# Which column pairs use the seven-product scheme, which PSUM banks they and their neighbours take, and where the input forms are built: one transformer kernel on one core

## The chip, the core and the metric

The kernel runs on one NeuronCore of a Trainium2 chip. Five engines work side by side: TensorE (PE, with its weight loads shown apart as PEld), VectorE (DVE), ScalarE (ACT), GpSimd (POOL) and SyncE (SP, here the queue that issues the weight transfers). Each runs its own instruction list in order and waits on semaphores for the others. PSUM has eight banks of 128 x 512 float32 words; a matmul writes into a bank, ACT and DVE read it out. The metric is the device time of one execution in microseconds (us), the median of several runs.

## The reference, cut to what matters

Two transformer blocks are computed on 512 tokens of width 1024, in float32. The change touches three of the SwiGLU feed-forward layers of the second block:

```python
def _swiglu(x, w_in, w_out):
    a, b = jnp.split(x @ w_in, 2, axis=-1)      # w_in: 1024 x 5632, a = gate, b = val
    return (jax.nn.silu(a) * b) @ w_out          # w_out: 2816 x 1024
# per layer l:
n = _modulate(_rmsnorm_2(h, norm_g[l, 0]), mod[:, 0, 0], mod[:, 0, 1])
h = h + 0.5 * mod[:, 0, 2] * _swiglu(n, ffn_w_in[l, 0], ffn_w_out[l, 0])
# ... the mixer ...
n = _modulate(_rmsnorm_2(h, norm_g[l, 2]), mod[:, 2, 0], mod[:, 2, 1])
h = h + 0.5 * mod[:, 2, 2] * _swiglu(n, ffn_w_in[l, 1], ffn_w_out[l, 1])
```

There are four such layers. The three that the change touches are called s01 (layer 0, second), s10 and s11 (layer 1, first and second).

## The kernel before, in words

**Number format.** Every float32 operand of a matmul is split into a high part and a rest (`HH`/`HL` for the layer's input, `AH`/`AL` for the activations, `wh`/`wl` for weights), and a product takes three matmuls: high x high, high x rest, rest x high. The weights come as slabs of 128 x 1024 (eight blocks of 128 x 128). SP loads slab n into one of five buffers `st`; `Act.split` copies it to `wh` (one of three), and `Dve.split` subtracts to get `wl`. Both are called by `spend`, two slabs ahead of TensorE, and `wh` of slab n waits until TensorE has used slab n-3.

**The up projection.** The 2816 columns of gate and val are taken in 22 groups g of 128, in 11 pairs p = 0 to 10 (g = 2p and 2p+1). In a plain pair, `linear` computes gate g, val g, gate g+1, val g+1, each one slab, 24 matmuls over all 512 tokens, into a bank of its own. ACT then takes the SiLU of gate (which frees gate's bank), DVE multiplies by val (which frees val's bank), ACT writes the high half to `AH`, DVE the rest to `AL`. Pair 0 is special: `three_linear` computes gate 0, val 0 and gate 1 together in two token halves, since the norm is still being finished, and then comes val 1.

**The fast pairs.** The pairs of `FAST` are computed by `fast_pair` with a Strassen-like scheme: columns g and g+1, and the even and odd 128-row blocks of the input, form a 2 x 2 block product in seven steps in place of eight, each step 24 matmuls over 256 words. The order is `FORMS`: 11, 12, s2, s1, s3, s4, 22. Its four weight slabs are combined by DVE sums (`Z`, and three sums in place in `st`) inside `Dve.split`. Four of the steps (s2, s1, s3, 22) need sums of the input, the input forms: `Dve.input_forms` builds `TF` 0 to 3 from the normalised input and then their rests `TL`, `Act.input_forms` the high parts `TH`. The results of gate and val gather in three banks each, by role: A (four steps), B (one), E (two). ACT copies partial results out (`kept`), DVE adds. The last output of a pair, from bank A, is finished by a closure `tail`, called by `finish_pair`, which frees the two A banks: gate's by a SiLU on ACT, val's by a product on DVE (line 2233).

**Halves.** `PARTS` = ((0, 12), (12, 10)): pairs 0 to 5, then a down projection over 12 groups, then pairs 6 to 10 and a down projection over 10 groups. Both down projections are eight plain linears over `AH`/`AL`.

**Banks.** `Pe.bank(key, ring)` takes the next bank of a ring, with one counter for each ring, which is never reset; `Pe.claim` makes TensorE wait until the bank's last holder is freed. Before, plain linears, the three of pair 0 and the down projection all use the ring (0, 1, 2, 3, 4), and fast pairs take six banks in turn from the ring 0 to 7. TensorE works in order, so a bank that is not free stops everything behind it.

**Order on DVE and ACT.** For each plain g, `fast_swiglu` does: `spend(8)` (not for g = 1), `finish_pair`, the forms where they are due, `spend(8)`, the SiLU or product, high half and rest. In g = 0 all four forms and their four rests stand around the second `spend`.

Of the kernel before, what the change touches and what calls it, by code (L numbers as in the profile page):

```python
# [19 lines left out]
DFF = 2816  # L20
# [2 lines left out]
NWS = 3  # L23
HID = 11
PARTS = ((0, 12), (12, 10))
FAST = (1, 3, 5, 7, 9)
FORMS = ("11", "12", "s2", "s1", "s3", "s4", "22")
NC = 8
RESET = 256
# [4 lines left out]
def c128(start):  # L34
    return np.arange(start, start + 128)
# [139 lines left out]
def finish(steps):  # L175
    for _ in steps:
        pass
# [277 lines left out]
class Pe:  # L455
# [590 lines left out]
    def fast_pair(self, key, p, up):  # L1046


        m, w = self.m, self.w
        g, n0, r0 = 2 * p, self.cur.at // 8, len(self.specs) // 8  # L1050
        for row, k in ((0, 0), (0, 1), (1, 0), (1, 1)):
            self.specs += [(*up, c128((2 * i + k) * 128), c128(at + (g + row) * 128)) for at in (0, DFF) for i in range(4)]
        self.plan += [(kind, r0) for kind in FORMS]
        self.freed += [("sum", n0 + 5), ("lo", n0 + 5), ("lo", n0 + 4), ("lo", n0 + 6)]
        self.cur.at += 56
        ring = tuple(range(8))

        def plain_form(k, h):
            return [[t[2 * i + k][:, part(h)] for i in range(4)] for t in (m.HH, m.HL)]

        def turned_form(t):
            w.wait_ge("form lo", key, t)
            return [[a[t][:, 256 * i:256 * i + 256] for i in range(4)] for a in (m.TH, m.TL)]

        for step, kind in enumerate(FORMS):
            n = n0 + step
            w.wait_ge("lo", n)
            s = n % NWS
            hi, lo = plain_form(*{"11": (0, 0), "12": (1, 0), "s4": (1, 1)}[kind]) if kind in ("11", "12", "s4") else turned_form(("s1", "s2", "s3", "22").index(kind))
            for x, name in enumerate(("gate", "val")):  # L1070
                bank = ("A", "B", "A", "E", "A", "E", "A")[step]
                out = (key, name, bank, g)
                if step in (0, 1, 3):
                    b = self.bank(out, ring)
                else:
                    b = m.ps[self.banks[out]]
                    w.wait_ge("kept", key, g, x, (None, None, 0, None, 1, 2, 3)[step])
                for i in range(4):
                    cols = slice(512 * x + 128 * i, 512 * x + 128 * i + 128)
                    wh, wl = m.wh[s][:, cols], m.wl[s][:, cols]  # L1080
                    self.mm(b[:, 0:256], wh, hi[i], i == 0 and step in (0, 1, 3), False)
                    self.mm(b[:, 0:256], wh, lo[i], False, False)
                    self.mm(b[:, 0:256], wl, hi[i], False, i == 3, *([("q", key, g, x, step)] if i == 3 else []), *([("used", n)] if x and i == 3 else []))

    def fast_ffn(self, key, after, up, down):
        m = self.m
        dense = (0, 1, 2, 3, 4)

        def one(name, g):
            finish(self.linear((key, name, g), fe(c128((0 if name == "gate" else DFF) + g * 128), *up, 8), m.HH, m.HL, None, dense))  # L1090

        for half, (first, count) in enumerate(PARTS):
            self.w.stamp("pe ffn", key, half)
            for p in range(first // 2, (first + count) // 2):
                if p == 0:
                    self.three_linear([(key, "gate", 0), (key, "val", 0), (key, "gate", 1)], [fe(c128(at), *up, 8) for at in (0, DFF, 128)], m.HH, m.HL, key, dense)
                    one("val", 1)
                elif p in FAST:
                    self.fast_pair(key, p, up)
                else:  # L1100
                    for g in (2 * p, 2 * p + 1):
                        one("gate", g)
                        one("val", g)
            if half:
                self.w.stamp("inputs free", after)
            for i in range(8):
                specs = [(down[0], down[1], c128((first + j) * 128), c128(i * 128)) for j in range(count)]
                ready = [("lo", key, "f", first + j) for j in range(count)]
                if half and i == 7:
                    self.last_linear((key, "down", half, i), specs, m.AH, m.AL, ready, dense, after)  # L1110
                else:
                    finish(self.linear((key, "down", half, i), specs, m.AH, m.AL, ready, dense))
            self.pad()

    def mixer(self, l):
# [229 lines left out]
class Act:  # L1345
# [590 lines left out]
    def fast_pair(self, key, p, j):  # L1936
        m, w, g = self.m, self.w, 2 * p

        def keep(step, k, bank):
            for x, name in enumerate(("gate", "val")):  # L1940
                w.wait_ge("q", key, g, x, step)
                self.act(m.kept[x][k], self.ps(key, name, bank, g)[:, 0:256], ACT.Copy, ("kept", key, g, x, k))

        for step in range(7):
            finish(self.spend(8))
            if step == 0:
                self.finish_pair()
            if step in (0, 2, 3, 4):
                keep(step, {0: 0, 2: 1, 3: 2, 4: 3}[step], "E" if step == 3 else "A")
        w.wait_ge("c1", key, g, 0)  # L1950
        self.act(m.c1[0], m.c1[0], ACT.Silu, (key, "silu", g))
        w.wait_ge(key, "f", g)
        self.half((key, "f", g), m.c1[0], m.AH[j])

        def tail():
            if g >= 2:
                w.wait_ge("lo", key, "f", g - 1)
            w.wait_ge("q", key, g, 0, 6)
            self.act(m.y2[:, part(0)], self.ps(key, "gate", "A", g)[:, 0:256], ACT.Silu, ("free", (key, "gate", "A", g)), scale=-1.0)
            w.wait_ge("c22", key, g, 0)  # L1960
            self.act(m.y2[:, part(1)], m.c22[0], ACT.Silu, (key, "silu", g + 1), scale=-1.0)
            w.wait_ge(key, "f", g + 1)
            self.half((key, "f", g + 1), m.y2, m.AH[j + 1])

        self.tail = tail

    def fast_swiglu(self, key, after, l, sub):
        m, w = self.m, self.w
        self.high_halves(key, self.shift(l, sub))
        forms = self.input_forms(key)  # L1970
        for half, (first, count) in enumerate(PARTS):
            for p in range(first // 2, (first + count) // 2):
                if half:
                    w.wait_ge("pe ffn", key, half)
                if p in FAST:
                    self.fast_pair(key, p, 2 * p - first)
                    continue
                for g in (2 * p, 2 * p + 1):
                    if g != 1:
                        finish(self.spend(8))  # L1980
                    self.finish_pair()
                    if g == 0:
                        next(forms)
                        next(forms)
                    finish(self.spend(8))
                    if g == 0:
                        finish(forms)
                    y = m.f[0 if g % 2 else 2]
                    w.wait_ge(key, "gate", g)
                    if g >= 2:  # L1990
                        w.wait_ge("lo", key, "f", g - 2)
                    self.act(y, self.ps(key, "gate", g), ACT.Silu, ("free", (key, "gate", g)), (key, "silu", g))
                    w.wait_ge(key, "f", g)
                    w.wait_ge("pe ffn", key, half)
                    self.half((key, "f", g), y, m.AH[g - first])
            self.finish_pair()
            self.down(after, half, count)
# [215 lines left out]
class Dve:  # L2213
# [714 lines left out]
            self.tail()  # L2928
            self.tail = None

    def fast_pair(self, key, p, j):
        m, w, g = self.m, self.w, 2 * p

        def summed(out, kept, x, name, bank, step, *points):
# [3 lines left out]

        for step in range(7):
            finish(self.spend(8))  # L2940
            if step == 0:
                self.finish_pair()
            for x, name in enumerate(("gate", "val")):
                if step == 1:
                    summed(m.c1[x][:, part(0)], 0, x, name, "B", 1)
# [20 lines left out]
    def fast_swiglu(self, key, after, l, sub):  # L2966
        m, w = self.m, self.w
        self.adanorm(key, l, sub)
        forms = self.input_forms(key, l, sub)
        for half, (first, count) in enumerate(PARTS):  # L2970
            for p in range(first // 2, (first + count) // 2):
                if p in FAST:
                    self.fast_pair(key, p, 2 * p - first)
                    continue
                for g in (2 * p, 2 * p + 1):
                    if g != 1:
                        finish(self.spend(8))
                    self.finish_pair()
                    if g == 0:
                        next(forms)  # L2980
                        next(forms)
                    finish(self.spend(8))
                    if g == 0:
                        finish(forms)
                    y = m.f[0 if g % 2 else 2]
                    w.wait_ge(key, "silu", g)
                    w.wait_ge(key, "val", g)
# [482 lines left out]
```

## Time and profile before

| | before |
|---|---|
| runs | 3354.31, 3357.98, 3357.48 us |
| median | 3357.48 us |
| profiled execution | 3356.16 us, span 3354.4 us |
| granted TensorE clock, mean | 0.992 |
| busy: PE / PEld / DVE / ACT / POOL | 98% / 81% / 60% / 41% / 4% of the span |

The span is the time from the first to the last instruction of the profiled execution. "Busy" is the union of an engine's instructions. A row of the wait or timeline views ends with the idle time before the instruction and, after an arrow, what ended it. PEclk, or granted clock, is the share of TensorE's full clock (2.4 GHz) that was granted; half of it is 1.2 GHz.

### The profile page before, as it was taken

What the parts mean: (1) busy time and instruction counts of PE and PEld (TensorE: products, weight loads), DVE (VectorE), ACT (ScalarE), POOL (GpSimd) and SP (SyncE); (2) the same over time, 40 slices, a digit from 0 to 9 for tenths busy, and PEclk for the clock granted to TensorE, in tenths of its full rate; (3) what the DMA queues carried; (4) which work ended last, traced back from release to release, by engine and by line L of the source; (5) the groups of instructions that cost most, each with busy time, mean ns of one, the idle gap of its engine ahead of it and who ended that gap; (6) DMA issues with size and microseconds to landing.
All of it is one profiled execution on the core that took longest, in us unless ns stands there. A gap on an engine that the chain in (4) does not pass through costs nothing.

```text
span 3354.4 us, 49836 instructions
## 1 busy us (share of the span) xinstructions
PE 3277.8 (98%) x21186; PEld 2730.3 (81%) x21186; DVE 2008.2 (60%) x3327; ACT 1391.4 (41%) x2352; POOL 118.7 (4%) x211
## 2 busy tenths in 40 slices
PE   8999999999999999999999899999999999999998
PEld 6878768888888888887778788889898877888897
DVE  6575764678576756566645654566364566475454
ACT  5234566345244422235543442344243455343242
POOL 1000000101000011100000000000000000000000
PEclk9999999999999999999999899999999999999999
DMA  4010103655543466632112132323333321222332
GB/s 153 25 58 30 39 32 122 217 175 202 181 139 132 151 217 212 224 131 94 45 64 94 63 109 93 101 65 106 113 101 121 100 68 45 84 80 76 113 101 69
DMA packets 101742, 364.28 MB, mean 109 GB/s; under 512 B 11776, under 2 KB 13888, under 8 KB 100880
## 3 DMA queue, kind: packets, MB, share of 16 engines
q1 hardware_dynamic: 77040, 272.14, 24.4%
q0 software_dynamic: 24480, 88.95, 7.8%
q8 instruction: 167, 2.74, 0.3%
q14 instruction: 55, 0.45, 0.0%
HBM read 358.94 MB, written 2.10 MB: 108 GB/s over the span
## 4 chain that ended last, share of the span: by engine, by line
PE 90%; DVE 6%; ACT 3%; issue 1%; DMA 0%; POOL 0%; DVEq 0%; ACTq 0%; POOLq 0%
PE ps_run L478 89%; PE ps_run L870 1%; DVE wl L2226 1%; ACT wh L1358 1%; ACT nrm L1358 1%; DVE TF L2233 0%; DVE TL L2226 0%; DVE nrm L2233 0%; PE ps_run L1208 0%; DVE HL L2233 0%; DVE msk L2230 0%; ACT bias L1358 0%; DVE nrm L2226 0%; DVE X L2233 0%; ACT HH L1358 0%
## 5 line engine op out<-in xcount | busy, mean ns | idle before, releaser
L2226 DVE TENSOR_TENSOR wl<-st,wh 128x1024 fp32r<-128x1024 f32 x541 | 658.8, 1218 | 654.3 <-ACT wh L1358 654.2
L478 PE MATMUL ps_run<-HH,wh 128*128 128x512 f32 (+1 forms) x2656 | 987.1, 372 | 44.0 <-DVE f L2226 12.0
L478 PE MATMUL ps_run<-HH,wl 128*128 128x512 f32 (+1 forms) x2656 | 966.6, 364 | 0.0
L478 PE MATMUL ps_run<-HL,wh 128*128 128x512 f32 (+1 forms) x2656 | 964.9, 364 | 0.0
L1358 ACT ACTIVATE wh<-st 128x1024 fp32r<-128x1024 f32 x541 | 566.2, 1048 | 648.7 <-PE ps_run L478 646.8
L478 PEld LDWEIGHTS ps_run<-HH,wh 128*128 128x128 f32 x2656 | 506.8, 191 | 133.3 <-DVE f L2226 13.1
L478 PEld LDWEIGHTS ps_run<-HH,wl 128*128 128x128 f32 x2656 | 506.3, 191 | 78.9
L478 PEld LDWEIGHTS ps_run<-HL,wh 128*128 128x128 f32 x2656 | 507.3, 191 | 77.6 <-issue 3.8
L478 PE MATMUL ps_run<-AH,wh 128*128 128x512 f32 (+1 forms) x1164 | 446.1, 383 | 1.3 <-ACT f L1358 1.3
L478 PE MATMUL ps_run<-AH,wl 128*128 128x512 f32 (+1 forms) x1164 | 440.3, 378 | 0.0
L478 PE MATMUL ps_run<-AL,wh 128*128 128x512 f32 (+1 forms) x1164 | 440.1, 378 | 0.0
L478 PEld LDWEIGHTS ps_run<-AH,wh 128*128 128x128 f32 x1164 | 218.9, 188 | 44.7 <-issue 2.6
L478 PEld LDWEIGHTS ps_run<-AL,wh 128*128 128x128 f32 x1164 | 219.0, 188 | 42.4 <-issue 1.9
L478 PEld LDWEIGHTS ps_run<-AH,wl 128*128 128x128 f32 x1164 | 218.9, 188 | 41.1
L2379 DVE CUSTOM_DVE_ANT_0 mb<-mb,mb 128x1024 f32<-128x1024 f32 x144 | 172.5, 1219 | 0.0
L1358 ACT ACTIVATE AH<-f 128x512 fp32r<-128x512 f32 x73 | 46.1, 632 | 280.3 <-DVE f L2226 261.1
L478 PE MATMUL ps_run<-TH,wh 128*128 128x256 f32 x480 | 136.0, 283 | 1.1 <-DVE wl L2226 1.1
L478 PE MATMUL ps_run<-TL,wh 128*128 128x256 f32 x480 | 135.8, 283 | 0.0
L478 PE MATMUL ps_run<-TH,wl 128*128 128x256 f32 x480 | 135.8, 283 | 0.0
L1358 ACT ACTIVATE nrm<-X 128x512 f32<-128x512 f32 (+1 forms) x72 | 42.0, 583 | 205.9 <-DVE X L2233 130.5
L1358 ACT ACTIVATE nrm<-ps_run 128x256 f32<-128x256 f32 (+3 forms) x180 | 77.1, 434 | 114.6 <-PE ps_run L478 92.8
L2233 DVE SCALAR_TENSOR_TENSOR X<-ps_run,mod,X 128x512 f32<-128x512 f32 (+1 forms) x86 | 61.2, 712 | 100.0 <-PE ps_run L478 99.9
(456 smaller groups left out, 4027.9 us busy)
## 6 DMA issues: line engine op xcount, KB each, us to landing
st<-wst SPq DMA_DIRECT2D x511, 512.0 KB, 3.5
mb<-ada POOLq DMA_DIRECT2D x144, 512.0 KB, 4.6
cw<-cw POOLq DMA_DIRECT2D x4, 1024.0 KB, 6.2
X<-xT SPq DMA_DIRECT2D x8, 256.0 KB, 5.9
X<-xT POOLq DMA_DIRECT2D x8, 256.0 KB, 4.7
out<-X SPq DMA_DIRECT2D x16, 128.0 KB, 1.8
kc<-kc POOLq DMA_DIRECT2D x1, 1073.5 KB, 6.9
mb<-cond POOLq DMA_DIRECT2D x2, 512.0 KB, 5.6
```

The source lines that it names most:

```text
L478: i = self.e.matmul(out, lhsT, rhs, start=start, stop=stop, skip_group_check=True)
L870: t = self.e.transpose(b[0:rows, kt * 128:(kt + 1) * 128], P[:, kt * 128:kt * 128 + rows], self.m.C("ident"))
L1358: self.e.activation(out, src, fn, **kw).then_inc(*self.w.done(*points))
L2226: self.e.tensor_tensor(out, a, b, op).then_inc(*self.w.done(*points))
L2233: self.e.scalar_tensor_tensor(out, a, s, b, op1, op2).then_inc(*self.w.done(*points))
L2379: self.e.tensor_tensor_reduce(slab, slab, m.mbuf[3], 1.0, 0.0, MUL, ADD, m.mod[l][:, j:j + 1]).then_inc(*w.done(("ada used", l, j)))
```

## The change

1. `FAST` goes from (1, 3, 5, 7, 9) to (2, 4, 6, 8, 10). There are five fast pairs either way. Pair 1 becomes plain, so pairs 0 and 1 stand plain in a row; the first half ends with a plain pair and the second begins and ends with a fast one.
2. Banks by role. A fast pair claims A at 0 and 1 (or 2 and 3 if p is odd, which no longer occurs), B at 4 and 5, E at 6 and 7 (gate first, then val). Plain linears of these layers use the ring (5, 6, 7), the down projection the ring (4, 5, 6). Only the first three linears of pair 0 keep (0, 1, 2, 3, 4).
3. Inside a fast pair `finish_pair` is called at step 2, not 0.
4. The forms are spread: on DVE the first two after the spends of g = 0, the next two ahead of g = 1's spend, three of the rests behind the spends of g = 1, 2 and 3, and the last at step 3 of pair 2. On ACT two high parts ahead of g = 1's spend and two ahead of g = 2's second spend.

```diff
-FAST = (1, 3, 5, 7, 9)
+FAST = (2, 4, 6, 8, 10)
@@ Pe.fast_pair
-        ring = tuple(range(8))
+        first = {"A": (0, 2)[p % 2], "B": 4, "E": 6}
@@
-                    b = self.bank(out, ring)
+                    b = self.claim(out, first[bank] + x)
@@ Pe.fast_ffn
-        dense = (0, 1, 2, 3, 4)
+        dense, plain, outputs = (0, 1, 2, 3, 4), (5, 6, 7), (4, 5, 6)
@@ one(name, g)
-            finish(self.linear(..., m.HH, m.HL, None, dense))
+            finish(self.linear(..., m.HH, m.HL, None, plain))
@@ down projection
-                    self.last_linear((key, "down", half, i), specs, m.AH, m.AL, ready, dense, after)
+                    self.last_linear((key, "down", half, i), specs, m.AH, m.AL, ready, outputs, after)
                 else:
-                    finish(self.linear((key, "down", half, i), specs, m.AH, m.AL, ready, dense))
+                    finish(self.linear((key, "down", half, i), specs, m.AH, m.AL, ready, outputs))
@@ Act.fast_pair
-            if step == 0:
+            if step == 2:
                 self.finish_pair()
@@ Act.fast_swiglu
                     self.finish_pair()
-                    if g == 0:
+                    if g in (1, 2):
                         next(forms)
                         next(forms)
                     finish(self.spend(8))
-                    if g == 0:
-                        finish(forms)
@@ Dve.fast_pair
-            if step == 0:
+            if step == 2:
                 self.finish_pair()
+            if step == 3:
+                finish(forms)
@@ Dve.fast_swiglu
-                    if g == 0:
-                        next(forms)
+                    if g == 1:
                         next(forms)
                     finish(self.spend(8))
-                    if g == 0:
-                        finish(forms)
+                    if g < 4:
+                        next(forms)
```

## Rows read from the trace of the kernel before

**Rows 1.** The page: busy time by engine, and the costliest ACT group.

```profile
PE 3277.8 (98%) x21186; PEld 2730.3 (81%) x21186; DVE 2008.2 (60%) x3327; ACT 1391.4 (41%) x2352; POOL 118.7 (4%) x211
...
L1358 ACT ACTIVATE wh<-st 128x1024 fp32r<-128x1024 f32 x541 | 566.2, 1048 | 648.7 <-PE ps_run L478 646.8
```

**Rows 2.** Busy time by stretch; columns: stretch, length, engines, granted clock, DMA.

```profile
1861.27:1991.85 130.58, 114.26 (x723) 104.74 (x721) 80.69 (x97) 56.73 (x85) 0.00 (x0) 0.93 0.27 86
2057.28:2167.03 109.75, 107.48 (x626) 95.60 (x624) 58.53 (x67) 42.57 (x63) 0.00 (x0) 0.98 0.29 96
2241.98:2359.83 117.85, 111.93 (x722) 102.74 (x721) 79.65 (x96) 55.45 (x82) 0.00 (x0) 0.97 0.28 94
2425.14:2530.78 105.64, 105.64 (x625) 94.37 (x624) 58.54 (x67) 42.58 (x63) 0.00 (x0) 1.00 0.31 101
2987.89:3117.84 129.95, 117.57 (x722) 106.38 (x721) 79.79 (x96) 55.54 (x82) 0.00 (x0) 0.93 0.26 85
3183.15:3288.79 105.64, 105.64 (x626) 94.37 (x624) 58.53 (x67) 42.58 (x63) 0.00 (x0) 1.00 0.31 100
2241.98:2247.45 5.47, 5.47 (x27) 4.51 (x25) 5.40 (x11) 5.12 (x5) 0.00 (x0) 1.00 0.00 0
2297.74:2317.89 20.15, 20.15 (x169) 20.14 (x168) 13.42 (x17) 10.98 (x17) 0.00 (x0) 1.00 0.40 132
2317.89:2339.68 21.79, 21.79 (x98) 18.03 (x97) 12.34 (x14) 7.45 (x11) 0.00 (x0) 1.00 0.20 73
```

**Rows 3.** Timeline of TensorE: the matmuls that ended seven of its waits.

```profile
1877.96 0.55 PE L478 MATMUL ps_run<-HH,wh 128*128 128x256 f32 x1 [11.06 <-DVE f L2226]
...
1904.98 0.80 PE L478 MATMUL ps_run<-HH,wh 128*128 128x512 f32 x1 [3.93 <-DVE f L2233]
...
1991.85 0.50 PE L478 MATMUL ps_run<-AH,wh 128*128 128x512 f32 x1 [1.33 <-ACT f L1358]
...
2143.56 0.80 PE L478 MATMUL ps_run<-HH,wh 128*128 128x512 f32 x1 [2.27 <-ACT f L1358]
...
2255.59 0.58 PE L478 MATMUL ps_run<-HH,wh 128*128 128x256 f32 x1 [5.11 <-DVE wl L2226]
...
3001.50 0.58 PE L478 MATMUL ps_run<-HH,wh 128*128 128x256 f32 x1 [4.20 <-DVE wl L2226]
...
3048.85 0.36 PE L478 MATMUL ps_run<-HH,wh 128*128 128x256 f32 x1 [0.94 <-DVE f L2226]
```

**Rows 4.** Timeline of DVE at the start of s10.

```profile
2238.92 1.22 DVE L2226 TENSOR_TENSOR TF<-even,even 128x1024 f32<-128x1024 f32 x1
2240.17 1.67 DVE L2233 SCALAR_TENSOR_TENSOR TF<-TF,mod,odd 128x256 f32<-128x256 f32 x4
...
2248.58 3.49 DVE L2226 TENSOR_TENSOR TL<-TF,TH 128x1024 fp32r<-128x1024 f32 x3
2251.99 0.68 DVE L2226 TENSOR_TENSOR f<-f,ps_run 128x512 f32<-128x512 f32 x1
2253.36 0.69 DVE L2226 TENSOR_TENSOR AL<-f,AH 128x512 fp32r<-128x512 f32 x1 [0.69 <-ACT AH L1358]
2254.31 1.23 DVE L2226 TENSOR_TENSOR wl<-st,wh 128x1024 fp32r<-128x1024 f32 x1 [0.25 <-ACT wh L1358]
```

**Rows 5.** Timeline of DVE and ACT around fast pair 1 of s01 and pair 2 of s11.

```profile
1897.83 0.80 DVE L2226 TENSOR_TENSOR nrm<-nrm,ps_run 128x256 f32<-128x256 f32 x2
...
1904.50 0.42 DVE L2233 SCALAR_TENSOR_TENSOR f<-ps_run,f 128x256 f32<-128x256 f32 x1
...
3032.65 0.58 ACT L1358 ACTIVATE f<-ps_run 128x512 f32<-128x512 f32 x1
...
3037.14 0.69 DVE L2226 TENSOR_TENSOR f<-f,ps_run 128x512 f32<-128x512 f32 x1 [3.13 <-PE ps_run L478]
```

**Rows 6.** Timeline of DVE and ACT at the end of fast pair 5 of s01, and an ACT high half.

```profile
1993.62 0.69 DVE L2226 TENSOR_TENSOR AL<-f,AH 128x512 fp32r<-128x512 f32 x1 [0.70 <-ACT AH L1358]
...
2252.70 0.63 ACT L1358 ACTIVATE AH<-f 128x512 fp32r<-128x512 f32 x1 [4.56 <-DVE f L2226]
```

More of the change, by code:

```diff
@@ L1086, in fast_ffn @@
         m = self.m
-        dense = (0, 1, 2, 3, 4)
+        dense, plain, outputs = (0, 1, 2, 3, 4), (5, 6, 7), (4, 5, 6)
         def one(name, g):
-            finish(self.linear((key, name, g), fe(c128((0 if name == "gate" else DFF) + g * 128), *up, 8), m.HH, m.HL, None, dense))
+            finish(self.linear((key, name, g), fe(c128((0 if name == "gate" else DFF) + g * 128), *up, 8), m.HH, m.HL, None, plain))
         for half, (first, count) in enumerate(PARTS):
@@ L2929, in finish_pair, with fast_pair @@
             self.tail = None
-    def fast_pair(self, key, p, j):
+    def fast_pair(self, key, p, j, forms):
         m, w, g = self.m, self.w, 2 * p
@@ L2972, in fast_swiglu @@
                 if p in FAST:
-                    self.fast_pair(key, p, 2 * p - first)
+                    self.fast_pair(key, p, 2 * p - first, forms)
                     continue
```

## The prediction, made before the changed kernel was run

> **What bounds the kernel now.** The page comes first: PE is busy for 98% of the span, DVE for 60%, ACT for 41% [rows 1]. So time is either TensorE's own work or the little in which it stands. I listed PE's waits by window, then cut the three fast feed-forward layers into stretches at the borders between kinds of matmul [rows 2]. The reader is to see there three clean units, in which PE never stops and the clock is 1.00: one plain linear takes 5.47 us, a fast pair 20.15, a plain pair 21.79. The first half from val 1 to the down projection (val 1, pairs 1 to 5) holds one linear, three fast and two plain pairs: 5.47 + 3 x 20.15 + 2 x 21.79 = 109.50 us. It really takes 130.58 in s01, 117.85 in s10, 129.95 in s11: 21.08, 8.35 and 20.45 too much. The second half (pairs 6 to 10) takes 105.64 in s10 and s11, at clock 1.00, and 109.75 in s01: 4.11 too much. In all 53.99 us are lost. Everything else in these layers already runs without a stop, so this is all that a rearrangement can win there.
>
> What the loss is made of shows in TensorE's timeline [rows 3]. First, at the start: PE waits 11.06 us in s01 for a product on DVE, 5.11 in s10 and 4.20 in s11 for the rest of a weight slab. Both stand behind the input forms on DVE: in g = 0 it works through forms and rests until 2252.0, only then comes g0's product, and the slab's rest from 2254.31 to 2255.54 [rows 4], where PE resumes at 2255.59. Second, at borders between a fast and a plain pair: 3.93 us for the tail's product on DVE (it ends at 1904.92, PE resumes at 1904.98), 2.27 for its SiLU, 0.94 for the product of the last plain group [rows 3, 5]. These are banks: the two ring counters drift against each other, so some pairs meet a bank whose holder is just finishing and others don't, which is why s10 has none of them. Third, after these waits the granted clock is below 1 (0.93 in the first halves of s01 and s11, 0.97 in s10 [rows 2]), that is, some stretches at 1.2 GHz. Twelve waits of TensorE in these stretches, of which seven stand in [rows 3], add to 36.8 us; the other 17 of the 54 are such slow matmuls. A wait thus costs about half as much again as it lasts.
>
> **The change, part by part.**
>
> *Fast pairs moved.* Five of eleven either way, so the matmuls are the same. The first half gets one fast pair less (+1.64 us), the second one more (-1.64). Net 0. The slabs, splits and sums are the same in number too: nothing added on DVE, ACT or SP.
>
> *Forms spread.* Their work stays (1.22 + 3 x 1.67 on DVE, rests 4 x 1.22, and four ACT copies of about 1.05 [rows 1, 4]); what changes is who stands behind them. I laid DVE's new order out from the durations, with zero at the start of val 1 (2241.98 in s10; in s01 and s11 the distances are the same). PE needs gate 2's slab at 5.5, val 2's at 10.9, gate 3's at 16.4, val 3's at 21.9, pair 2's first at 27.3. DVE has gate 2's rest at about -0.3 (ACT's copy needs the `wh` that pair 0 gives back one slab before its end, 24 matmuls of 20.15 / 168 = 0.12 us or 2.9 before zero; then 1.05 and 1.23). Forms 0 and 1 (2.9) end at 2.7. g0's product, high half and rest (0.69 + 0.63 + 0.69, [rows 4, 6]) end at 4.8. Forms 2 and 3 (3.3) end at 8.1. Val 2's rest (1.23) ends at 9.3: 1.6 us before PE wants it. This is the narrowest place. Then a form's rest until 10.5, g1's product, high half and rest until 12.6, gate 3's `wl` 14.0 (2.4 to spare), val 3's about 17.1 (4.8 to spare; ACT's two copies of forms stand ahead of its `wh`), pair 2's first 21.8 and its `Z` 23.0 (4 to spare). The last rest falls in step 3 of pair 2 and is wanted at step 6, 8.6 us later; DVE is busy for only 13.42 of a fast pair's 20.15 [rows 2]. So no wait remains at the start: -11, -5, -4 and their slow matmuls. If the cover of 1.6 us is gone (one more DVE operation of 1.2 us would nearly do it), val 2 waits in each of three layers.
>
> *Banks by role.* Plain linear after fast pair: it takes 5, 6 or 7. These were B or E of the fast pair. The later, E, is read by DVE's two additions that end at 1898.63, 2.4 us before that pair's last matmul ends (1901.05) [rows 5], while A, freed 3.9 us after it, is no longer in the plain ring. So the 3.93 and 2.27 go. Fast after plain: A is 0 and 1, which no plain linear holds; the 0.94 goes, and the 11.06 too (it was A claiming val 1's bank). B comes at step 1, 2.9 us in, E at 8.6 us; the last val's product is out 0.94 + some tenths after the border. After a down projection the same holds, since its output is read within 1.5 us of its end. Inside a plain pair the second val takes the bank of the first gate: claimed at 16.4, freed by a SiLU that ended 8.9 us after the pair's start (3024.30 to 3033.23 [rows 5]): 7 us to spare. Gate 3 takes val 1's: freed at about 11.2, claimed at 16.4.
>
> *A new wait.* I counted the ring (4, 5, 6): 17 claims a layer, so it begins at 4, 6 and 5 in the three layers; the plain ring has 21, so val 11 is always in 5. In s11 the first down linear claims 5 just as val 11 ends, and must wait for its product: the 0.94 of the row above, once. Behind it stands only PE. It could be 0.7 (the product is idle-free) to 1.7 (with slow matmuls); I take 0.9.
>
> *Pair 10 fast before the second down projection.* After pair 5 of s01 the last rest `AL` ended at 1994.31 [rows 6], 3.8 us after the pair's last matmul (1991.85 less the wait of 1.33 [rows 3]); the down linear reaches its tenth block after 9 x 0.68 = 6.1. Nothing, with 2.3 us to spare.
>
> *Tails two steps later.* A tail pending at the start of a fast pair needs two fast pairs in a row, which neither set has (5 and 7, or 4 and 6, are separated by a pair or by a down projection that finishes the tail). Exactly 0.
>
> **The sum.** 3356.16 (profiled) - 53.99 + 0.94 = 3303.1. The median of the runs, 3357.48, is 1.3 above the profiled execution, which makes 3304.4 beside it; I give 3304.
>
> **A rule against it.** From rows, a claim in the ring of three comes 16.4 us after the claim it repeats, and the release at about 9 or 14 [rows 5]. The Trainium skill says otherwise for a ring this small: "Perfetto Trace Analysis", Matmul Optimizations, wants all 8 PSUM banks in use, and its Consistent bubbles (Optimization Strategy) reads a repeating gap as too few buffers. By the rows' sum that is worth 0; by the rule, rival 2. No row before has such a ring, so the trace does not settle it.
>
> **The rivals.**
>
> 1. *The forms still reach PE.* ACT and DVE hand over to each other with 0.25 to 0.69 us between [rows 4], and my chain has some six hand-overs before val 2's slab; if each costs a little more, 1.6 is used up. Then PE waits 1 to 3 us in each layer and some of it is paid again at 1.2 GHz: 3 x 1.5 to 3 x 4.5, so 3308 to 3317; middle 3311. Against it: the copies of ACT are ahead of DVE in my chart, and only two are waited for.
> 2. *Three banks are too few.* Every plain pair meets a late release. 15 plain pairs at the 0.94 of a product's release give 14 us: 3317. For: nothing but the ring's size. Against: the 7 us to spare.
> 3. *Slower.* The same mechanism deep enough: it would have to cost more than 54 / 15 = 3.6 us in each plain pair, so the SiLU or product would have to free its bank at 16.4 + 3.6 = 20 us after the pair's start, not at 9 or 14. From 3.6 on it decides; at 5 us, 3378. The plain group's chain has two splits per linear at most 2.3 us each in 5.47 us, so I see nothing that would push it there.
> 4. *The change moves the waits only.* If the forms' 12 us on DVE were simply late again in pair 1 or 2, PE would stand for them there; then only the bank waits at borders go: 3.93 and 2.27 in s01 and again in s11, 1.33, 0.94 and one of 0.68, in all 15.4, times 54 / 36.8 for the slow matmuls is 23, so 3333. Against: the chart's DVE has idle time before each slab.
>
> **How the numbers follow.** Forecast 0.76; rival 1 0.13; rival 2 0.05; rival 4 0.03; rival 3 and other losses 0.02; within 0.2% 0.01. The forecast's own spread: the 0.94 taken as 0 to 1.7, the 1.3 between profile and median, the spread of the runs (3.7): 3301 to 3307. To hold 8 in 10 I reach into rival 1: 3300 to 3313. A change of 0.2%, 6.7 us, is about what a measurement here can tell from none. Faster 0.96, same 0.02, slower 0.02.
>
> **What would show it.** In the changed kernel: val 1 to the down projection at 5.47 + 3 x 21.79 + 2 x 20.15 = 111.1 us in all three layers, the second half 104.0, clock 1.00 in both; no wait of PE over 1 us in them except about 0.9 before s11's first down linear, ended by DVE's `f` (2226); val 2's `wl` ending about 1.6 us before its first matmul. A wait ended by `wl` at val 2 or gate 3 is rival 1; one ended by ACT `f` inside plain pairs is rival 2; a wait at pair 2 ended by `TL` or `wl` is rival 4. A first half above 113 us would mean that a step of the sum is wrong.

## The result, and the profile after

The changed kernel takes 3304.43 us (median of 4 runs, 3302.09 to 3305.09). The kernel before, on the same chip, takes 3355.89 (3353.92 to 3357.98, four runs; three of them gave the 3357.48 ahead of the prediction). The ratio is 0.9845, with a 95% interval from 0.9828 to 0.9862. The profiled execution of after took 3304.45 us, with a span of 3302.7.

The page of after, its busy line and the group that answers to [rows 1]:

```profile
PE 3261.8 (99%) x21186; PEld 2719.0 (82%) x21186; DVE 2007.9 (61%) x3327; ACT 1390.7 (42%) x2352; POOL 118.7 (4%) x211
...
L1358 ACT ACTIVATE wh<-st 128x1024 fp32r<-128x1024 f32 x541 | 566.1, 1048 | 619.1 <-PE ps_run L478 616.8
```

Counts and durations of the operations are those of before: 541 copies of 1048 ns, 3327 instructions on DVE for 2008 us. Only TensorE's busy time has fallen, by 16 us (and that of its weight loads by 11), which are its slow matmuls. The rest of the gain is idle time.

The stretches that answer to [rows 2] (stretch, length, busy PE, PEld, DVE, ACT and POOL with counts, granted clock, DMA share and GB/s), in the order first and second half of s01, of s10, of s11, and then val 1 with pair 1 of s01:

```profile
1862.46:1973.56 111.10, 111.10 (x650) 98.89 (x649) 71.84 (x88) 49.11 (x72) 0.00 (x0) 1.00 0.33 105
2038.84:2142.88 104.04, 104.04 (x698) 96.51 (x697) 64.46 (x76) 47.41 (x72) 0.00 (x0) 1.00 0.33 106
2217.86:2328.96 111.10, 111.10 (x650) 98.88 (x649) 71.85 (x88) 49.11 (x72) 0.00 (x0) 1.00 0.32 104
2394.24:2498.28 104.04, 104.04 (x698) 96.51 (x697) 64.46 (x76) 47.41 (x72) 0.00 (x0) 1.00 0.33 107
2955.47:3067.59 112.12, 111.27 (x651) 98.71 (x649) 72.53 (x89) 49.15 (x73) 0.00 (x0) 1.00 0.33 104
3133.02:3237.05 104.03, 104.03 (x697) 96.50 (x696) 64.45 (x76) 47.41 (x72) 0.00 (x0) 1.00 0.32 107
...
1862.46:1889.69 27.23, 27.23 (x123) 22.54 (x122) 22.20 (x30) 12.34 (x16) 0.00 (x0) 1.00 0.25 78
```

In five of the six halves, length and busy PE are the same number: TensorE stands nowhere. The clock is 1.00 in all six. The fifth line, the first half of s11, holds the one wait that is left. It is in TensorE's timeline:

```profile
3067.59 0.50 PE L478 MATMUL ps_run<-AH,wh 128*128 128x512 f32 x1 [0.85 <-DVE f L2224]
```

It is all that is left where [rows 3] had waits of 11.06, 3.93, 2.27, 5.11, 4.20 and 0.94 us.

DVE at the start of s01, which answers to [rows 4] (start, duration, operation):

```profile
1862.27 1.22 DVE L2224 TENSOR_TENSOR TF<-even,even 128x1024 f32<-128x1024 f32 x1
1863.53 1.67 DVE L2231 SCALAR_TENSOR_TENSOR TF<-TF,mod,odd 128x256 f32<-128x256 f32 x4
1865.12 0.68 DVE L2224 TENSOR_TENSOR f<-f,ps_run 128x512 f32<-128x512 f32 x1
1866.50 0.69 DVE L2224 TENSOR_TENSOR AL<-f,AH 128x512 fp32r<-128x512 f32 x1 [0.70 <-ACT AH L1358]
1867.11 1.67 DVE L2231 SCALAR_TENSOR_TENSOR TF<-odd,dsh,even 128x256 f32<-128x256 f32 x4
1868.81 1.67 DVE L2231 SCALAR_TENSOR_TENSOR TF<-TF,mod,odd 128x256 f32<-128x256 f32 x4
1870.40 1.22 DVE L2224 TENSOR_TENSOR wl<-st,wh 128x1024 fp32r<-128x1024 f32 x1
```

The forms (`TF`) now stand in two groups with the product and rest of g0 between them. Val 2's `wl` ends at 1871.62. Val 2's first matmul is due 10.9 after 1862.46, at 1873.4: 1.7 us to spare.

### The profile page after: what moved, and what is told of

Read it like the earlier page. It is cut to its first block, busy times and chain, and to the rows that moved or that the text cites. A ratio compares the mean times of both kernels' runs of the same rounds, so it can differ in the third digit from the quotient of the medians.

```text
span 3302.7 us, 49851 instructions
## 1 busy us (share of the span) xinstructions
PE 3261.8 (99%) x21186; PEld 2719.0 (82%) x21186; DVE 2007.9 (61%) x3327; ACT 1390.7 (42%) x2352; POOL 118.7 (4%) x211
## 4 chain that ended last, share of the span: by engine, by line
PE 93%; DVE 4%; ACT 2%; issue 0%; DMA 0%; POOL 0%; DVEq 0%; ACTq 0%; POOLq 0%
PE ps_run L478 91%; PE ps_run L870 1%; DVE wl L2224 1%; ACT nrm L1358 1%; ACT wh L1358 0%; DVE nrm L2231 0%; PE ps_run L1208 0%; DVE HL L2231 0%; DVE msk L2228 0%; ACT bias L1358 0%; DVE X L2231 0%; ACT HH L1358 0%; DMA vec<-vec 0%; DVE L L2454 0%; DVE kn L2231 0%
## 5 line engine op out<-in xcount | busy, mean ns | idle before, releaser
L1358 ACT ACTIVATE wh<-st 128x1024 fp32r<-128x1024 f32 x541 | 566.1, 1048 | 619.1 <-PE ps_run L478 616.8
```

The costliest lines, as they stand in the source:

```text
L1358: self.e.activation(out, src, fn, **kw).then_inc(*self.w.done(*points))
```

## The experiments

All times are medians beside runs of the kernel before on the same chip (3354.6 to 3355.6 there); the edits are made to the changed kernel unless said otherwise. A line `...` in an edit marks code left out. The start of s01 lies between 1860.16 and 1862.46 in the executions of runs 1 to 7 and of the changed kernel, although no edit touches what stands before it; a difference of 2 us between two times is therefore read from the stretches, where they show it.

**1. Banks by role alone**, in the kernel before.

```
-        ring = tuple(range(8))
+        first = {"A": (0, 2)[p % 2], "B": 4, "E": 6}
...
-                    b = self.bank(out, ring)
+                    b = self.claim(out, first[bank] + x)
...
-        dense = (0, 1, 2, 3, 4)
+        dense, plain, outputs = (0, 1, 2, 3, 4), (5, 6, 7), (4, 5, 6)
...
```

`plain` and `outputs` are then used where the change uses them.

> The kernel before with nothing but the banks by role (fast pairs still 1, 3, 5, 7, 9, forms still built together in the first group). Theory (two separate causes: bank meetings at the borders, and the forms on DVE at the start): the border waits of s01 and s11 go, some 24 us with their slow matmuls; at the start of each layer the wait for the forms stays at what s10 had (8.4 us), so the three layers lose 3 x 8.4 to 3 x 9.5. Time 3327 to 3332. Rival (banks are the whole of it): about 3304.

Measured: 3329.43 us (3328.62 to 3331.08), ratio 0.9925 [0.9909, 0.9942]. The first halves of the three layers (the unit sum for this order is 109.50):

```profile
1861.19:1979.04 117.85, 113.12 (x722) 103.41 (x721) 79.65 (x96) 55.48 (x82) 0.00 (x0) 0.97 0.28 94
2226.10:2344.51 118.41, 111.11 (x723) 102.31 (x721) 79.66 (x96) 55.59 (x82) 0.00 (x0) 0.97 0.29 94
2972.64:3090.49 117.85, 111.67 (x722) 102.48 (x721) 79.64 (x96) 55.47 (x82) 0.00 (x0) 0.99 0.28 94
```

Each layer keeps 8.4 to 8.9 us, all of it at the start, where the forms still stand together; every wait at a border between pairs is gone. Only a new one of 0.84 us, behind DVE's `X`, stands between the first down projection of s01 and pair 6 (at 2045.36): a plain pair there claims a bank from which DVE has not yet read the down projection's output. The banks alone are worth 26 of the 51 us. They are worth more in s01 and s11 (130.58 and 129.95 before) than in s10, which had no waits at its borders before; in s01 the wait at the start was also longer. The first fast pair still meets banks of pair 0: 7.30 us behind ACT's `f` in s10 (at 2239.02, the bank of gate 1), and 0.67 and 2.77 us behind ACT's and DVE's `f` in s01. In s10 this adds little, since the forms held TensorE about as long: 8.9 us against 8.35 before.

**2. The old rings**, with everything else as in the changed kernel.

```
-        first = {"A": (0, 2)[p % 2], "B": 4, "E": 6}
+        ring = tuple(range(8))
...
-                    b = self.claim(out, first[bank] + x)
+                    b = self.bank(out, ring)
...
-        dense, plain, outputs = (0, 1, 2, 3, 4), (5, 6, 7), (4, 5, 6)
+        dense = plain = outputs = (0, 1, 2, 3, 4)
```

> The changed kernel with the banks of before (rings 0 to 4 and 0 to 7). From the rings' counters: a plain pair meets a bank A that the fast pair ahead of it has not freed at pair 3 of s01, pairs 7 and 9 of s10 and pair 5 of s11, a fast pair meets the last val at pairs 4 and 8 of s10; at 3.95 us for a gate's bank, 5.4 for val's (pair 9 of s10), 0.94 for the last val, less the one wait of the changed kernel (1.0): 18 us more, 3322. Start of each layer without a wait. Rival (the move of the pairs and forms did everything): 3304, within 2 us.

Measured: 3320.52 us (3319.56 to 3321.84), ratio 0.9897 [0.9883, 0.9912]. TensorE's waits, from its timeline (a second one of 0.94, at 2445.34, is left out):

```profile
1911.05 0.50 PE L478 MATMUL ps_run<-HH,wh 128*128 128x512 f32 x1 [2.27 <-ACT f L1358]
...
2291.05 0.36 PE L478 MATMUL ps_run<-HH,wh 128*128 128x256 f32 x1 [0.94 <-DVE f L2224]
...
2420.93 0.80 PE L478 MATMUL ps_run<-HH,wh 128*128 128x512 f32 x1 [2.27 <-ACT f L1358]
...
2469.66 0.80 PE L478 MATMUL ps_run<-HH,wh 128*128 128x512 f32 x1 [3.93 <-DVE f L2231]
...
3063.21 0.50 PE L478 MATMUL ps_run<-HH,wh 128*128 128x512 f32 x1 [2.27 <-ACT f L1358]
```

Sizes and releasers are the three kinds of [rows 3] (2.27, 0.94, 3.93), in new places, since the order of fast and plain pairs has changed. All six stand at the pairs that the count of the rings' claims named before the run. A wait of a given size is a given pair of holder and claimer; where it falls is arithmetic on the ring's counter. The plain pairs behind the three waits of 2.27:

```profile
1911.05:1934.54 23.49, 23.49 (x96) 19.26 (x97) 10.85 (x12) 5.55 (x8) 0.00 (x0) 0.93 0.17 48
2420.93:2445.34 24.41, 23.46 (x97) 19.04 (x97) 11.54 (x13) 5.67 (x9) 0.00 (x0) 0.94 0.14 47
3063.21:3085.12 21.91, 21.91 (x96) 18.13 (x97) 7.36 (x9) 5.56 (x8) 0.00 (x0) 1.00 0.32 97
```

The same wait costs 1.7 us more where the clock falls behind it (23.49 against the clean 21.79, clock 0.93) and 0.1 more where it doesn't (21.91, clock 1.00). The 24.41 of the second holds a wait of 0.94 besides.

**3. The forms together**, as before, with the new banks and the new order of pairs. The edit on DVE; ACT's high parts go back to g = 0 likewise.

```
-                    if g == 1:
+                    if g == 0:
+                        next(forms)
                         next(forms)
                     finish(self.spend(8))
-                    if g < 4:
-                        next(forms)
+                    if g == 0:
+                        finish(forms)
```

> The changed kernel with all forms and their rests built in group 0, as before; pair 1 is plain still and banks are by role. DVE is then at val 2's rest at 12.8 us after the start of val 1, and PE wants it at 10.9: a wait of 1.9 us in each layer, ended by wl, and up to 1.5 more each if the clock falls: 3310 to 3315, middle 3312. Rival (the extra plain pair covers all, the spreading is worth nothing): 3304.

Measured: 3307.97 us (3307.23 to 3308.84), ratio 0.986 [0.9845, 0.9874]. Below the range that I gave. The wait is where it was expected, in each of the three layers, but it is 1.5 us and not 1.9, and no slow matmuls follow; in s01 and s11:

```profile
1872.74 0.47 PE L478 MATMUL ps_run<-HH,wh 128*128 128x512 f32 x1 [1.51 <-DVE wl L2226]
...
2969.33 0.47 PE L478 MATMUL ps_run<-HH,wh 128*128 128x512 f32 x1 [1.50 <-DVE wl L2226]
```

Val 1 with pair 1 of s01, as a stretch:

```profile
1860.16:1889.19 29.03, 27.52 (x123) 22.46 (x121) 22.39 (x27) 14.01 (x17) 0.00 (x0) 1.00 0.23 73
```

That is 1.8 us longer than the 27.23 of the changed kernel, and the same in each layer (29.03, 29.03, 28.99), 5.4 in all. The medians differ by only 3.5; in the profiled execution s01 starts 2.3 us earlier than in the changed kernel's (1860.16 against 1862.46), which accounts for the difference. So spreading the forms is worth 5.4 us once the pair after val 1 is plain. Most of what the forms cost before came from pair 1 being fast: with the forms together and pair 1 fast the start costs 8.4 to 8.9 us a layer (run 1), with pair 1 plain 1.8. Runs 1 and 3 were timed on the same chip and differ in the order of the pairs alone (the tail's step acts in neither): 3329.43 against 3307.97, 21.5 us (25.6 us too much at the three starts in run 1, 5.4 here). A fast pair wants its slabs 2.9 us apart, a plain one 5.47.

**4 and 5. One and three more operations on DVE** ahead of val 2's slab, in each layer; their result is overwritten before anything reads it. The edit with one; with three, the range is 3.

```
                     if g == 1:
                         next(forms)
+                        for _ in range(1):
+                            w.own()
+                            self.tt(m.Z, m.TF[0], m.TF[1], ADD)
```

> The changed kernel with one addition of 1.22 us more on DVE in group 1 ahead of val 2's split (three of them brought a wait of 2.0 us). The margin is 1.7, so nothing should wait: 3304, within 2 us, and the first halves at 111.1 us. Rival (the margin is smaller than the trace says): a wait ended by wl at val 2 in each layer, 3306 to 3309.

> The changed kernel with three additions of 128 x 1024 more on DVE (written to Z, read by nobody) in group 1, between the forms and val 2's split. Each is 1.22 us, 3.7 in all; the margin there is 1.7 in the trace (the rest ends at 1871.62, val 2 starts 10.9 after 1862.46). So val 2 waits 2.0 us in each layer, and up to 1.5 more each if the clock falls: 3310 to 3315. Rival (margin is larger since other things give way): 3304 to 3307.

One operation: 3303.01 us (3302.13 to 3303.36), ratio 0.9841 [0.9828, 0.9855], and no wait at val 2. Three: 3312.75 us (3310.43 to 3312.86), ratio 0.9872 [0.9858, 0.9887]. The margin lies between 1.2 and 3.7 us; three operations of 1.22 less the margin read above (1.7) is 2.0, and that is the wait. Val 1 with pair 1 in the three layers (27.23 undisturbed), and the wait in the first and the third:

```profile
1862.17:1891.69 29.52, 27.51 (x123) 22.45 (x121) 25.05 (x32) 12.35 (x16) 0.00 (x0) 1.00 0.24 72
2219.86:2249.39 29.53, 27.51 (x123) 22.45 (x121) 25.06 (x32) 12.35 (x16) 0.00 (x0) 1.00 0.23 72
2959.76:2990.89 31.13, 29.11 (x123) 23.58 (x121) 25.88 (x33) 12.35 (x16) 0.00 (x0) 0.95 0.23 68
```

```profile
1875.25 0.47 PE L478 MATMUL ps_run<-HH,wh 128*128 128x512 f32 x1 [2.01 <-DVE wl L2224]
...
2972.85 0.47 PE L478 MATMUL ps_run<-HH,wh 128*128 128x512 f32 x1 [2.02 <-DVE wl L2224]
2973.15 0.59 PE L478 MATMUL ps_run<-HL,wh 128*128 128x512 f32 x1
```

The waits are alike to 0.01 us, yet one is followed by matmuls of 0.59 and costs 3.9 us, the others 2.3.

**6. Two banks for the plain linears** in place of three.

```
-        dense, plain, outputs = (0, 1, 2, 3, 4), (5, 6, 7), (4, 5, 6)
+        dense, plain, outputs = (0, 1, 2, 3, 4), (5, 6), (4, 5, 6)
```

> The changed kernel with a ring of two banks (5, 6) for plain linears in place of three. Theory: what counts is how long before its claim a bank is freed. With two banks gate g+1 takes gate g's bank 10.9 us after the pair's start, freed at 8.9; val g+1 takes val g's at 16.4, freed at about 13; so no wait inside plain pairs. With 21 claims a layer the last val sits in 5, 6, 5, and the first down linear claims 4, 6, 5: one 0.9 us wait more, in s10. Time 1 us above the changed kernel, 3304 to 3307. Rival (few banks starve TensorE): waits in each of the 15 plain pairs, 3310 and above.

Measured: 3305.96 us (3304.63 to 3307.26), ratio 0.9855 [0.984, 0.987]. Plain pairs keep their 21.79, val 1 with pair 1 takes 0.3 longer (27.57, 27.53 and 27.52 in the three layers), and the 0.85 before the first down linear now also stands in s10:

```profile
2328.67 0.50 PE L478 MATMUL ps_run<-AH,wh 128*128 128x512 f32 x1 [0.85 <-DVE f L2224]
```

By the stretches that makes 2 us. Even two banks are nearly enough, so three are not scarce: rival 2 is out.

**7. Other banks for the down linears**, which no pair's last linear holds.

```
-        dense, plain, outputs = (0, 1, 2, 3, 4), (5, 6, 7), (4, 5, 6)
+        dense, plain, outputs = (0, 1, 2, 3, 4), (5, 6, 7), (2, 3, 4)
```

> The changed kernel with the down projection's ring at (2, 3, 4) in place of (4, 5, 6), so that its first linear never meets the last val. The wait of 0.85 us before the first down linear of s11 goes (with what follows, 1.2 us: first half 111.1 in all three layers); nothing else moves. 3302 to 3304. Rival (the wait is for the product's rest, not for a bank): it stays.

Measured: 3302.34 us (3301.31 to 3303.61), ratio 0.9844 [0.983, 0.9859]. The wait of 0.85 is gone and all three first halves take 111.1. That the time is better than the changed kernel's is not shown, since the runs overlap; where the wait came from is.

**8. All of pairs 2 to 10 fast.** The layer's budget of fast pairs was five; each further one saves 21.79 - 20.15 = 1.64 us of matmuls.

```
-FAST = (2, 4, 6, 8, 10)
+FAST = (2, 3, 4, 5, 6, 7, 8, 9, 10)
```

> The changed kernel with all pairs but 0 and 1 fast (2 to 10). Each of the 4 x 3 more replaces 21.79 by 20.15 us of TensorE: 19.7 us less, and the wait of s11 goes too: 3284 if nothing waits. DVE has some 18.8 of 20.15 us of work in each pair (11 passes of 1.22, the additions, products and rests). Rival (DVE or the slab loads cannot follow from pair to pair): PE waits at each border of two fast pairs by 0.5 to 2 us, ended by wl, 21 borders: 3295 to 3325.

Measured: 3327.77 us (3324.33 to 3329.73), ratio 0.9919 [0.9904, 0.9934]: 23 us slower than the changed kernel and 43 above the sum without waits. That is outside both ranges, but the rival's mechanism is there: waits at the borders ended by `wl`, 24.2 us in all (one of 0.69 stands inside a pair). The first border of a run of fast pairs costs 0.16 us of waiting; of the fifteen later ones nine cost 1.8 to 2.1, one 2.9 and five 0.2 to 0.7. The rest of the 43 us is in slower matmuls behind the waits: of the 9.5 us that the first run of four pairs is above 4 x 20.15, 5.64 are waited and 3.86 are matmuls. DVE around the second border of s01, and the matmul that waited:

```profile
1921.84 1.23 DVE L2224 TENSOR_TENSOR wl<-st,wh 128x1024 fp32r<-128x1024 f32 x1 [0.80 <-ACT wh L1358]
...
1928.09 1.23 DVE L2224 TENSOR_TENSOR Z<-st,st 128x1024 f32<-128x1024 f32 x1 [1.61 <-DMA st<-wst]
...
1935.94 1.23 DVE L2224 TENSOR_TENSOR wl<-st,wh 128x1024 fp32r<-128x1024 f32 x1 [0.26 <-ACT wh L1358]
```

```profile
1937.22 0.39 PE L478 MATMUL ps_run<-TH,wh 128*128 128x256 f32 x1 [1.86 <-DVE wl L2224]
```

The slab for which TensorE waits is late because DVE's `Z` had waited 1.61 us for a transfer. DVE isn't full: it is busy for 68.65 of the 90.10 us of this run of four pairs.

**9 to 11. The same with the tail at step 0, 1 and 3** instead of 2 (on ACT and on DVE; the edit for step 0).

```
-            if step == 2:
+            if step == 0:
                 self.finish_pair()
```

> The same with the tail at step 0, as before the change. In the changed kernel this edit never acts; here it acts at seven borders in each layer. On ACT the tail's high half waits for DVE's product (behind a rest and a sum, about 4.4 us into the pair) and kept 0 and the next wh queue behind it: kept 0 is wanted at 5.8. If that is close enough, waits of 0 to 1 us ended by ACT nrm or wl at steps 2 and 3, 0 to 21 us in all above the kernel with step 2; if not, the same time.

> As the kernel with pairs 2 to 10 all fast, but the tail at step 1 instead of step 2 (at step 0 it was 3392.75, at step 2 3327.77). If the tail's distance from the border is what costs, the time lies between the two: each step of distance took 32 us on average, so about 3360, with waits of TensorE behind ACT's nrm or a slab's wl. If step 0 was a threshold, because only there the SiLU waits for the last sum behind the slab work, it is 3320 to 3330, as at step 2.

> As the kernel with pairs 2 to 10 all fast (3327.77, 21 borders between fast pairs), but the tail of the pair before is issued at step 3 instead of step 2. Two readings of the 1.9 us waits of TensorE at the borders. (a) The tail itself is in the way: at the second border of a run ACT's SiLU and high half and DVE's product (1933.61) and rest (1935.00) stand ahead of the slab's wl (1935.94 to 1937.17) for which TensorE waits; then the wait leaves its place and the kernel gets faster by most of the 43 us that it is above the waitless sum, or the wait turns up one slab later (2.9 us) with another size. (b) The slabs are late in themselves: DVE's Z waited 1.61 us for a transfer at 1928.09, before the tail; then the waits stay in size, 3325 to 3331. Where the tail stands must then hardly matter. I expect a mixture: 3300 to 3325, nearest to 3315.

Step 0: 3392.75 us (3392.12 to 3393.09), ratio 1.0114 [1.0097, 1.0131]. Step 1: 3314.47 (3312.01 to 3316.09), ratio 0.9878 [0.9862, 0.9895]. Step 3: 3293.77 (3292.47 to 3296.13), ratio 0.9818 [0.9804, 0.9833]. All three fell outside what I expected. TensorE's wait lines in the three fast layers, for step 0, 1 and 3 (releaser: us in total, times, longest):

```profile
PE ps_run L478 <- ACT nrm L1358: 66.7, 22, 4.0
```

```profile
PE ps_run L478 <- DVE wl L2224: 19.6, 40, 2.9
```

```profile
PE ps_run L478 <- DVE wl L2224: 5.5, 21, 0.3
```

At step 0 ACT's tail stands ahead of the copies that give the new pair's banks back, and 3.11 us are waited at 20 borders and 4.00 at one (the 22nd wait of this line, 0.41 us at 2684.74, stands between the layers). At step 3 the waits are 0.16 at a run's first border and 0.30 later. DVE at the same border of s01, tail at step 3:

```profile
1919.12 1.22 DVE L2224 TENSOR_TENSOR wl<-st,wh 128x1024 fp32r<-128x1024 f32 x1 [0.41 <-ACT wh L1358]
...
1926.15 1.22 DVE L2224 TENSOR_TENSOR Z<-st,st 128x1024 f32<-128x1024 f32 x1
```

The tail's two products stand behind this split of a slab and no longer ahead of it: it ends at 1920.34, where it ended at 1923.07 with the tail at step 2. `Z` finds its data, and the whole chain behind it is 1.9 us earlier (0.3 of it because this run of pairs starts 0.3 earlier). So the tail's place is the cause of the waits of run 8, which was my reading (a). That the late split held a staging buffer, and so started the next transfer late, fits both timelines; no run changes the number of these buffers, so that link is argued. Nor do I know why step 1 lies below step 2; the traces show only where: at step 1 two waits at borders are over 1.5 us (2.92 and 1.76), at step 2 ten.

**12. Seven fast pairs, in runs of at most two.**

```
-FAST = (2, 4, 6, 8, 10)
+FAST = (2, 3, 5, 6, 7, 9, 10)
```

> The changed kernel with seven fast pairs, never more than two in a row (2, 3, 5 | 6, 7, 9, 10), so that a plain pair or the down projection follows each run of two. With all nine fast the first border of a run cost 0.16 us and the second 1.8 to 2.0. Theory (DVE falls behind a little in each fast pair and needs a plain pair to catch up): two more fast pairs in each of three layers, 6 x 1.64 = 9.8 us less, the bank wait of s11 (1.2 with what follows) goes, and 9 borders of 0.16 are paid: 3304.4 - 9.8 - 1.2 + 1.4 = 3295. Rival (any two fast pairs in a row cost 2 us): 9 x 2, 3311 or more.

Measured: 3297.59 us (3296.68 to 3298.76), ratio 0.9826 [0.9813, 0.9839], 6.8 us below the changed kernel. The first run of two:

```profile
1889.13:1929.97 40.84, 40.68 (x338) 40.42 (x337) 32.83 (x41) 22.41 (x37) 0.00 (x0) 1.00 0.32 108
```

It takes 40.84 and not 2 x 20.15 = 40.30: 0.16 waited at the border and the rest in matmuls behind it. There are nine such runs, 4.9 us where 1.4 was expected, which is why it is 3297.6 and not 3295. The best time of all is that of run 11, all nine pairs fast with the tail at step 3: 3293.77, which is 10.7 us below the changed kernel.

## Why the prediction was right, point by point

Forecast 3304, measured 3304.43.

**The loss of 54 us, and that it all goes.** Right. The first halves were to be 111.1 and the second 104.0; they are 111.10, 111.10, 112.12 and 104.04, 104.04, 104.03. The one above is the new wait.

**The new wait at s11's first down linear.** Right in place, releaser and size: 0.85 us (the stretch is 1.02 too long), where 0.9 was taken and 0.94 stands in [rows 3]. Run 7 shows that it is for a bank which the plain linears hold too; that this is bank 5 is the count, and the count also placed the second such wait, in s10, of run 6.

**The forms.** The chart put the narrowest place at val 2 with 1.6 us to spare; it is 1.7, confirmed by runs 4 and 5. Rival 1 thus had the right place but not the size: six hand-overs didn't cost 1.7 us more. What the prediction did not separate is how much of the start came from the forms' place and how much from moving the first fast pair to pair 2. Run 3 says: 5.4 us of the gain hang on the spreading, the rest of the start is had by the new order of the pairs and the banks. The prediction costed the move of the fast pairs at nothing by its matmuls; in the sum that is right, but the move carried most of the gain that was written down to the forms: 21.5 us between runs 1 and 3. No run spreads the forms with pair 1 still fast, so what the spreading alone would give there is not shown.

**The banks.** Right, and shown both ways: alone they give 26 us (run 1), and without them 16 are lost (run 2). The two differ since the waits of the old ring fall elsewhere with other pairs fast. Rival 2 fell with run 6. The Trainium skill, in "Perfetto Trace Analysis", Matmul Optimizations, asks for all 8 PSUM banks; here a ring of three for the plain linears costs nothing inside plain pairs and one of two 1.5 us by the medians, whose runs overlap, so the measurement decides against it for the plain linears of this kernel. The Trainium skill, in the same page, Optimization Strategy, says of consistent bubbles that a repeating gap can mean too few buffers; the gap that repeats at the borders in run 8, 1.8 to 2.1 us at nine of them, went to 0.3 or less with the same buffers in run 11. Rival 3, which needed the same mechanism in more depth, fell with it; rival 4 needed waits at pair 2, and there are none.

**Tails two steps later: exactly 0.** Right for the changed kernel, in which no two fast pairs meet. Runs 8 to 11 show what stands behind the edit: as soon as they do, the tail's step decides over 99 us (3392.75 at step 0, 3293.77 at step 3). The change took step 2, and step 3 would be the better one to build on.

**A wait costs half as much again as it lasts.** This is the ratio of the sum it was read from (54 against 36.8), and no rule for one wait. Waits of 1.5 us and less in the fast layers never had slow matmuls behind them in runs 3, 6 and 12. Waits of 2.0 to 2.3 had them once in three (run 5) and twice in three (run 2), at 1.6 to 1.7 us more each time, and the nine of 1.8 to 2.1 in run 8 seven times. The slow matmuls that it allowed put the middle of my range for run 3 at 3312; the lower end, 3310, had none. The three layers cost 5.4 us, which gives 3309.8, and the profiled execution fell below that by the 2.3 us ahead of s01. Nothing of it touched the forecast, because all the waits but one went.

**Against the profiled time.** The sum gave 3303.1 for the execution whose span I read; that of after took 3304.45. The six stretches add to 646.43 where the sum has 646.36, which accounts for 0.1 of the 1.3. Another 1.2 was there before s01 began: its first half starts at 1862.46, and at 1861.27 in [rows 2]. The change doesn't reach that part, so this is the difference between two executions. The forecast then added 1.3 for a median above the profiled execution, which was not there: after's median is 3304.43 beside 3304.45, and with its fourth run that of before is 3355.89 beside 3356.16. The two cancel, so the agreement to 0.4 us is luck; that of the stretches is not.

## What to carry to other kernels

When TensorE is nearly always busy, cut its timeline into units that repeat, take the cleanest of each as the unit's price, and the sum of the excess is all that reordering can win; the releasers then tell which of it a given edit gets. Give banks by who holds them and when they are released, not by a shared counter: a ring whose period doesn't match the pattern puts the same wait in another place each layer, and its size is not its scarcity (two banks did nearly what three do). Work that is handed to the helpers late, like the tail here, belongs behind the splits that the next pair needs first; here step 3 was the best of the four tried, and the times of the others follow no simple order.

## What the runs showed of the hardware

The granted clock doesn't follow the length of a wait alone. Three waits of 2.01 to 2.02 us in one execution had clock 1.00, 1.00 and 0.95 over the stretch in which they stand, and three of 2.27 had 0.93, 0.94 and 1.00 over the pair behind them, between the same kinds of matmuls; each of these three falls to the lower level (1.2 GHz) cost 1.5 to 1.7 us. In run 8 two waits of 1.92 us at two borders in a row show the same; the pairs behind them:

```profile
3199.93:3220.44 20.51, 20.51 (x168) 20.25 (x168) 16.23 (x21) 9.58 (x18) 0.00 (x0) 1.00 0.33 103
3222.36:3244.25 21.89, 21.89 (x168) 21.69 (x168) 17.31 (x22) 11.06 (x21) 0.00 (x0) 0.92 0.31 97
```

The Trainium skill, "TensorE: Matmul & The Clock Gate", Part 1, calls the chip's view of activity free-running, which would make the same wait count or not by when it falls. These runs agree with that.
